# A hybrid decoder layer on one core: the mixer phase's mask cut in parts, its exponentials in three groups, the SSD step size moved into the exponent, and the gated norm split between w_out and ScalarE

## The chip, the cores and the metric

The kernel runs on one core of a Trainium2 chip. The metric is the device time of one execution in microseconds. The kernel before takes 3205.09 us in the median of three runs (3201.73 to 3206.28).

## What is computed

One decoder layer over 2048 tokens of width 1024 in float32. A combined projection feeds three token mixers: S5 (512 channels), Mamba-2 SSD (768 channels, 12 heads of 64, two B/C groups) and mLSTM (6 heads, key width 64, value width 128). Their outputs are concatenated (2048 wide), multiplied by `w_out`, normed and added to x, and a SwiGLU feed-forward follows. What the change touches is this:

```python
dt = softplus(dt_raw + dt_bias)
xdt = x * dt[..., None]
acs = cumsum(dt * a)                       # within a chunk of 128
decay = exp(where(causal, acs[l] - acs[s], -inf))
y_diag = einsum(cb, decay, xdt)            # cb = C B^T of the chunk
...
y = y_diag + y_off + x * d_skip
y = y * silu(z)
y = rmsnorm(y, norm_g)                     # over each of two groups of 384 channels
mix = concat[y_a, y_b, y_c] @ w_out
```

The mLSTM part has a causal matrix of exponentials of the same kind for its six heads.

## The kernel before, in words

The layer is five phases, one after the other, with a barrier between them: channels, tokens, mixers, out and feed-forward. Every float32 product of the big projections is made of three products of operands split in an upper and a lower part: ScalarE copies the upper part in a rounded type, VectorE subtracts it from the whole to get the lower part, and TensorE multiplies upper by upper, lower by upper and upper by lower.

**Tokens (`phase_tokens`).** TensorE runs through units of weights; each is loaded by SyncE, split by ScalarE (`upper`, L924) and VectorE (`lower`, L1003) and multiplied (L1126). At fixed slots between them `gates` computes the gates of the mixers for a quarter of the tokens, so four times in all: VectorE L1021 to L1054, ScalarE L941 to L952 (Exp and Ln), VectorE L1057 and L1058, then TensorE's transposes L1143. The row `col_b` (L1047) holds minus the cumulated decay of each head, and goes to the mixers as a column of `tok_cols`.

**Mixers (`phase_mixers`).** The 2048 tokens are 16 chunks of 128, with one loop over chunks written out by hand on every engine; semaphores count chunks. The order of work on each queue is the order in the code.

- SyncE loads for chunk c the rows `bc` (L1289, 18 rows of 128 numbers, spread to all partitions), `ch` (L1294), `va` (L1295), `tk` (L1297) and `zo` (L1300) into buffer c mod 2. All five raise one semaphore, `in_[b]`; each load waits for what its buffer was read by two chunks before: `bc` for the mLSTM product, `zo` for `y_ok`. Then, in the first three chunks, two pieces of `w_out` (L1305).
- GpSimd makes `xde` (L1402) and `xskip` (L1405), waits for VectorE's `off_read`, adds (L1407), makes `ve` (L1410), and adds the causal mask to all 18 heads of the next chunk in one instruction (`masked`, L1393), after a wait for all five loads.
- ScalarE copies three upper parts of the transposed y of the chunk before (`upper_y`, L1341), squares and sums y (L1326), takes the root by Ln and Exp (L1333, L1334), computes the 18 exponentials of the next chunk (`exponentials`, L1320), sends y, and moves out a finished product (L1354).
- VectorE waits for all exponentials, multiplies them by the products (L1449 for mLSTM, L1454 for SSD), makes `xdt` (L1457), scales the old states (L1458, L1459), reads the product with the old state (L1466), adds (L1474) and gates (L1475) the SSD output, updates states (L1479, L1495), forms the mLSTM output (L1482, L1490, L1498 to L1500, L1504 for six heads) and ends with the norm of y by root and gain (L1508, two instructions). Between these it makes the lower parts of the transposed y (`lower_y`, L1428), and in the first three chunks those of `w_out` (`lower_w`, L1422).
- TensorE has the products of the chunk (L1554 qk, L1560 cb, L1566 off, L1575 diag, L1583 state, L1591 inter, L1599 pv, L1606 c), twelve transposes of the chunk before (L1543), and between them in pieces the 36 matmuls of the projection of the chunk two before with half of `w_out` (`project`, L1529).

The order of TensorE around VectorE's exponent products:

```python
pe.wait_ge(gm_ok, 2 * c + 2)     # L1449, both
... off products, project(c - 2, 3, 4), transposes(c - 1, 0), project(c - 2, 4, 6)
pe.wait_ge(g_ok, 2 * c + 2)      # L1454, both
pe.wait_ge(xdt_ok, c + 1)
... diag products
```

**Out (`phase_out`).** It loads the rest of `w_out` in five groups of four row tiles into two buffers (L1652), splits them (L1711 on ScalarE, L1774 on VectorE), and multiplies (L1814); each group's load waits until the lower part of the group two before is made.

## Time and profile before

| what | value |
| --- | --- |
| median of three runs | 3205.09 us |
| time of the profiled execution | 3212.2 us |
| its span, first to last instruction | 3210.4 us |
| TensorE busy | 2919.7 us, 91% |
| VectorE busy | 1959.8 us, 61% |
| ScalarE busy | 1167.8 us, 36% |
| GpSimd busy | 372.4 us, 12% |
| mean granted TensorE clock | 0.955 |

Times are microseconds from the first instruction. PE is TensorE (PEld its weight load), DVE VectorE, ACT ScalarE, POOL GpSimd; a q behind a name is the engine's queue of issued DMAs. Where a row gives three numbers with slashes, they are the shortest, the median and the longest duration in ns. In a timeline a row is: start, duration, engine, line, operation, what it writes and reads, shape, count, and in brackets the idle time before it with what ended it. The mixers lie between about 1153 and 1635 us, tokens end at 1153, out begins at 1635. The profiled execution takes 1.8 us more than its span and 7.1 us more than the median.

### The profile page before, as it was taken

The numbers are of one execution on the slowest core, as the hardware profiler recorded it, in microseconds if no ns is written. First come the engines' busy times: TensorE is split into PE (matmuls) and PEld (weight loads), VectorE is DVE, ScalarE is ACT, GpSimd is POOL, SyncE is SP. The second block draws the span as 40 slices with busy tenths as digits, with TensorE's granted clock in tenths as the row PEclk, the third lists the DMA queues.
The fourth block names the chain that finished last, engine by engine and source line by source line (L and its number), as shares of the span: only waits on it lengthen the run. The fifth ranks groups of instructions, "written<-read, shape, count | busy, mean of one in ns | idle before, by whom it ended". The sixth has DMA issues, their size and how long they took to land. (4 is left out here: it accounts for less than half of the span.)

```text
span 3210.4 us, 35825 instructions
## 1 busy us (share of the span) xinstructions
PE 2919.7 (91%) x13608; PEld 2346.8 (73%) x13608; DVE 1959.8 (61%) x2603; ACT 1167.8 (36%) x1917; POOL 372.4 (12%) x415
## 2 busy tenths in 40 slices
PE   7999999789997846888869968999999999999998
PEld 4888887577775535666648856888878888888887
DVE  3777887556632218887823437676777655665756
ACT  5222222443433323333323334333343333354543
POOL 0000000004420014444401210000000000000000
PEclk9999999889998878999979988999999999999999
DMA  4222442336655455675456856344454222586863
GB/s 142 63 76 85 138 132 82 124 128 214 211 176 141 126 179 180 210 244 206 170 213 249 332 190 226 151 154 157 155 189 172 111 102 99 183 292 195 290 194 114
DMA packets 289959, 545.51 MB, mean 170 GB/s; under 512 B 58460, under 2 KB 150012, under 8 KB 276348
## 3 DMA queue, kind: packets, MB, share of 16 engines
q1 hardware_dynamic: 258028, 438.08, 40.5%
q0 software_dynamic: 24704, 75.52, 6.5%
q10 hardware_dynamic: 7056, 29.63, 2.3%
q8 instruction: 108, 1.77, 0.2%
q14 instruction: 63, 0.52, 0.1%
HBM read 358.69 MB, written 184.44 MB: 169 GB/s over the span
## 5 line engine op out<-in xcount | busy, mean ns | idle before, releaser
L2344 PE MATMUL f_banks<-f_bop,f_w_op 128*128 128x512 f32 x3696 | 840.4, 390 | 31.6 <-DVE f_w_op L2171 29.4
L2344 PEld LDWEIGHTS f_banks<-f_bop,f_w_op 128*128 128x128 f32 x3696 | 694.9, 188 | 177.1 <-DVE f_w_op L2171 29.8
L2352 PE MATMUL f_banks<-f_d_op 128*128 128x512 f32 x1848 | 419.0, 389 | 0.0
L2352 PEld LDWEIGHTS f_banks<-f_d_op 128*128 128x128 f32 x1848 | 347.0, 188 | 71.9
L1126 PE MATMUL t_banks<-t_w_hi,h_hi 128*128 128x512 f32 (+1 forms) x640 | 250.8, 392 | 31.9 <-DVE t_w_lo L1003 31.9
L2235 DVE TENSOR_TENSOR f_d_op<-f_d_raw,f_d_op 128x1024 fp32r<-128x1024 f32 x154 | 187.5, 1225 | 148.9 <-ACT f_d_op L2088 148.2
L639 PE MATMUL c_banks<-h_hi,c_w_hi 128*128 128x512 f32 x640 | 255.8, 400 | 0.0
L639 PE MATMUL c_banks<-h_hi,c_w_lo 128*128 128x512 f32 x640 | 249.9, 390 | 0.0
L639 PE MATMUL c_banks<-h_lo,c_w_hi 128*128 128x512 f32 x640 | 249.1, 389 | 0.0
L1126 PE MATMUL t_banks<-t_w_hi,h_lo 128*128 128x512 f32 (+1 forms) x640 | 240.8, 376 | 0.0
L1126 PE MATMUL t_banks<-t_w_lo,h_hi 128*128 128x512 f32 (+1 forms) x640 | 240.2, 375 | 0.0
L2088 ACT ACTIVATE f_d_op<-f_d_raw 128x1024 fp32r<-128x1024 f32 x154 | 162.9, 1061 | 198.3 <-PE f_banks L2352 161.6
L2070 ACT ACTIVATE f_snap<-f_banks 128x1024 f32<-128x1024 f32 x88 | 90.3, 1026 | 260.3 <-PE f_banks L2344 260.3
L1126 PEld LDWEIGHTS t_banks<-t_w_hi,h_hi 128*128 128x128 f32 x640 | 124.2, 194 | 64.0 <-DVE t_w_lo L1003 33.6
L894 POOL DMA_DIRECT2D tokmaj<-t_out x96 | 52.9, 553 | 980.5 <-ACT t_out L931 980.3
L2171 DVE TENSOR_TENSOR f_w_op<-f_w_sum,f_w_op 128x1024 fp32r<-128x1024 f32 x66 | 80.8, 1225 | 129.4 <-ACT f_w_op L2058 128.5
L1814 PE MATMUL o_banks<-o_w_hi,o_y_hi 128*128 128x512 f32 x320 | 129.3, 404 | 24.0 <-DMA o_y_lo<-y_lo 16.3
L1003 DVE TENSOR_TENSOR t_w_lo<-t_raw,t_w_hi 128x2048 fp32r<-128x2048 f32 x36 | 82.5, 2292 | 109.5 <-ACT t_w_hi L924 109.0
L418 DVE SCALAR_TENSOR_TENSOR c_arena<-c_row,c_cw,c_arena 128x512 f32<-128x512 f32 x192 | 144.3, 752 | 6.8
L1126 PEld LDWEIGHTS t_banks<-t_w_hi,h_lo 128*128 128x128 f32 x640 | 124.6, 195 | 23.5 <-issue 3.8
L1126 PEld LDWEIGHTS t_banks<-t_w_lo,h_hi 128*128 128x128 f32 x640 | 124.3, 194 | 21.6
L2171 DVE TENSOR_TENSOR f_w_op<-f_raw,f_w_op 128x1024 fp32r<-128x1024 f32 x88 | 107.8, 1225 | 52.4 <-ACT f_w_op L2058 50.2
(341 smaller groups left out, 4660.5 us busy)
## 6 DMA issues: line engine op xcount, KB each, us to landing
f_raw<-in_w_gu SPq DMA_DIRECT2D x88, 512.0 KB, 6.5
sop<-f_a SPq DMA_DIRECT2D x154, 256.0 KB, 2.0
f_d_raw<-sop SPq DMA_DIRECT2D x154, 256.0 KB, 2.9
t_raw<-in_w_tok SPq DMA_DIRECT2D x36, 1024.0 KB, 5.6
f_d_raw<-top SPq DMA_DIRECT2D x88, 256.0 KB, 4.1
m_bc<-rows SPq DMA_DIRECT2D x16, 1152.0 KB, 6.8
f_d_raw<-in_w_dn SPq DMA_DIRECT2D x66, 256.0 KB, 3.0
o_y_hi<-y_hi SPq DMA_DIRECT2D x16, 1024.0 KB, 5.0
```

The costliest lines, as they stand in the source:

```text
L418: ins = nc.vector.scalar_tensor_tensor(conv[:, s], row[:, s, k:NB + k], cw[:, m, k:k + 1], conv[:, s], ALU.mult, ALU.add)
L639: last = nc.tensor.matmul(banks[:, p % RING, :], w[:, n % 2, k, :], h[:, k, q * NB:(q + 1) * NB], start=k == 0 and j == 0, stop=k == KD - ...
L894: pool.dma_start(tokmaj_dram[tile * P:(tile + 1) * P, to:to + width], out[:, e % 2, first:first + width]).then_inc(out_sent[e % 2], 16)
L1003: tt(w_lo[:, unit % 2], raw[:], w_hi[:, unit % 2].bitcast(F32), sub).then_inc(wlo_ok, 1)
L1126: last = nc.tensor.matmul(banks[:, t, 0:width], h[:, k_first + k, tok], w[:, unit % 2, cols], start=begins and k == 0 and j == 0, stop=end ...
L1814: last = nc.tensor.matmul(banks[:, b, half, :], y[:, b, ky, :], w[:, k, :], start=ky == 0 and j == 0, stop=k in (KM - 1, KM + WG - 1) and ...
L2070: nc.scalar.activation(snap[:, slot], bank, ACT.Copy).then_inc(snap_ok, 1)
L2088: nc.scalar.activation(d_op[:, d % D_RING, 0:2], d_raw[:, d % S_RING], ACT.Copy).then_inc(dhi_ok, 1)
L2171: tt(w_op[:, t % W_RING, 1], src, w_op[:, t % W_RING, 0].bitcast(F32), sub).then_inc(wlo_ok, 1)
L2235: tt(d_op[:, d % D_RING, 2:4], d_raw[:, d % S_RING], d_op[:, d % D_RING, 0:2].bitcast(F32), sub).then_inc(dlo_ok, 1)
L2344: last = nc.tensor.matmul(bank[:, g, :], w_op[:, t % W_RING, w, cols], bop[:, s, h, k, :], start=begins and k == 0 and j == 0, stop=k == 3 ...
L2352: last = nc.tensor.matmul(banks[:, bank, :], d_op[:, d % D_RING, s, tok], d_op[:, d % D_RING, w, :], start=k == 0 and j == 0, stop=k == FU ...
```

## The change

In the tokens phase the SSD rows of `col_b` become ln(dt) minus the cumulated decay, so that the exponential holds the step dt and `xdt` is not made. In the mixers `bc` has a semaphore of its own, the mask is added in six instructions of three heads, ScalarE computes the exponentials in three groups at three places, the gain of the norm is multiplied into rows of `w_out` while these are split, and ScalarE multiplies y by the root.

```diff
@@ phase_tokens, ScalarE (r == 6), VectorE (r == 0) and (r == 7)
+                    chain(nc.scalar.activation(x[s_, :], x[s_, :], ACT.Ln))
                     chain(nc.scalar.activation(col_b[f, :], x[f, :], ACT.Exp))
...
+                    chain(ts(x[s_, :], sp_[s_, :], TINY, None, ALU.max))
                     chain(nc.vector.tensor_copy(decay[:, tiles], end))
...
+                    chain(tt(col_b[s_, :], x[s_, :], cum[s_, :], sub))
                     chain(ts(col_c[f, :], col_c[f, :], DK ** -0.5, None, mul))
@@ phase_mixers
-LOADS = 5
+LOADS = 4
+MH = 3
+MASKED = (12, 15, 0, 3, 6, 9)
+GK = XW // P
@@ SyncE
-            ... (gain[:], norm_gain.partition_broadcast(P)),
+            ... (gain[:], norm_gain),
-                             rows_dram[c]...partition_broadcast(P)).then_inc(in_[b], 16)
+                             rows_dram[c]...partition_broadcast(P)).then_inc(bc_in[b], 16)
@@ ScalarE
             def upper_w(g):
                 act.wait_ge(w_in[g % 2], 16 * (g // 2 + 1))
-                nc.scalar.activation(w_hi[:, WM * g:WM * (g + 1), :], w_raw[:, g % 2], ACT.Copy).then_inc(whi_ok, 1)
+                if WM * g < GK:
+                    for k in range(WM * g, WM * (g + 1)):
+                        ins = nc.scalar.activation(w_hi[:, k, :], w_raw[:, g % 2, k % WM], ACT.Copy, scale=gain[:, k:k + 1])
+                else:
+                    ins = nc.scalar.activation(w_hi[:, WM * g:WM * (g + 1), :], w_raw[:, g % 2], ACT.Copy)
+                ins.then_inc(whi_ok, 1)
             def exponentials(c, first, last):
-                act.wait_ge(mask_ok, c + 1)
                 for h in range(first, last):
+                    if h % MH == 0:
+                        act.wait_ge(mask_ok, NBC // MH * c + MASKED.index(h) + 1)
@@ norm(c), behind its wait for mean_ok
                 chain(nc.scalar.activation(stat[:, 2, :], stat[:, 1, :], ACT.Ln))
-                nc.scalar.activation(stat[:, 3, :], stat[:, 2, :], ACT.Exp, scale=-0.5).then_inc(rstd_ok, 1)
+                chain(nc.scalar.activation(stat[:, 3, :], stat[:, 2, :], ACT.Exp, scale=-0.5))
+                for g in range(NG):
+                    at = y[:, c % 2, g * GW:(g + 1) * GW]
+                    ins = nc.scalar.activation(at, at, ACT.Copy, scale=stat[:, 3, g:g + 1])
+                ins.then_inc(yn_ok, 1)
@@ ScalarE's loop over chunks
                     upper_y(c - 1, 0)
                     upper_y(c - 1, 1)
+                if c + 1 < TT:
+                    exponentials(c + 1, HS, NBC)
+                if 1 <= c <= TT:
                     upper_y(c - 1, 2)
+                if c < TT:
+                    squares(c)
+                if c + 1 < TT:
+                    exponentials(c + 1, 0, HG)
                 if c < TT:
                     norm(c)
                 if c + 1 < TT:
-                    exponentials(c + 1, 0, HS)
-                    exponentials(c + 1, HS, NBC)
+                    exponentials(c + 1, HG, HS)
@@ GpSimd
             def masked(c):
-                pool.wait_ge(in_[c % 2], (c // 2 + 1) * 16 * LOADS)
-                nc.gpsimd.tensor_tensor(bc[:, c % 2], bc[:, c % 2], mask[:]..., ALU.add).then_inc(mask_ok, 1)
+                pool.wait_ge(bc_in[c % 2], (c // 2 + 1) * 16)
+                for h in MASKED:
+                    part = bc[:, c % 2, h:h + MH]
+                    nc.gpsimd.tensor_tensor(part, part, mask[:]..., ALU.add).then_inc(mask_ok, 1)
...
+                pool.wait_ge(in_[b], (c // 2 + 1) * 16 * LOADS)
@@ VectorE
-                dve.wait_ge(expo_ok, 2 * c + 2)
+                dve.wait_ge(expo_ok, 3 * c + 1)
...
                 for g in range(NG):
+                    dve.wait_ge(expo_ok, 3 * c + 2 + g)
...
-                tt(xdt[:], x, over(col(c, 0, 0, HS), HD), mul).then_inc(xdt_ok, 1)
...
-                dve.wait_ge(rstd_ok, c + 1)
-                for g in range(NG):
-                    at = slice(g * GW, (g + 1) * GW)
-                    ins = stt(y[:, b, at], y[:, b, at], stat[:, 3, g:g + 1], gain[:, at], mul, mul)
@@ TensorE: transposes wait for yn_ok (n == 0) and y_ok (n == 1); diag reads tk in place of xdt
-                pe.wait_ge(xdt_ok, c + 1)
@@ phase_out: SyncE, between the loads of y and of w_out's second group
+            sp.dma_start(norm_col[:], norm_gain).then_inc(norm_in, 16)
```

VectorE's `lower_w` is cut in the same way as `upper_w`: for the first three of six groups one scalar_tensor_tensor of 128x512 for each row tile, raw times gain minus upper. In `phase_out` the row tiles 4 to 9 carry the gain, so groups 1 and 2 (of 0 to 4) are split by four instructions of 128x512 each on ScalarE and on VectorE, and group 1 waits for the column of gains.

## Rows read from the trace of the kernel before

**Rows 1.** Windows, chunks 3 to 14: stretch, busy PE, PEld, DVE, ACT, POOL; clock, DMA

```profile
1283.20:1590.10 306.90, 257.78 (x1584) 200.67 (x1584) 254.18 (x348) 109.14 (x337) 138.84 (x60) 0.93 0.62 217
```

**Rows 2.** Timeline of PE, ACT and DVE at the mixers' first chunk

```profile
1190.53 1.65 PE L1554 MATMUL m_bank_x<-m_ch 64*128 64x128 f32 x12 [36.94 <-DMA m_zo<-tokmaj]
1195.71 5.36 ACT L1320 ACTIVATE m_bc<-m_bc,m_tok_cols 128x128 f32<-128x128 f32 x18 [28.36 <-POOL m_bc L1393]
1201.21 1.02 DVE L1449 SCALAR_TENSOR_TENSOR m_bc<-m_bc,m_bank_x 128x384 f32<-128x384 f32 x2 [33.69 <-ACT m_bc L1320]
```

**Rows 3.** Timeline of DVE: L1449 of chunks 3 and 15, chunk 8; all L1493

```profile
1283.17 1.02 DVE L1449 SCALAR_TENSOR_TENSOR m_bc<-m_bc,m_bank_x 128x384 f32<-128x384 f32 x2 [0.44 <-ACT m_bc L1320]
...
1417.35 0.96 DVE L1466 TENSOR_TENSOR m_off<-m_bank_x,m_tok_cols 128x768 f32<-128x768 f32 x1
...
1421.35 1.17 DVE L1475 TENSOR_TENSOR m_y<-m_y,m_zo 128x768 f32<-128x768 f32 x1
...
1427.67 2.56 DVE L1493 TENSOR_SCALAR m_stat<-m_stat 128x2 f32<-128x2 f32 x1
...
1430.72 0.94 DVE L1498 SCALAR_TENSOR_TENSOR m_den<-m_num 128x6 f32<-128x6 f32 x1
1431.69 1.40 DVE L1499 TENSOR_TENSOR m_den<-m_den,m_tok_cols 128x6 f32<-128x6 f32 x1
...
1433.35 2.29 DVE L1504 SCALAR_TENSOR_TENSOR m_y<-m_num,m_den,m_zo 128x128 f32<-128x128 f32 x6
1435.67 1.27 DVE L1508 SCALAR_TENSOR_TENSOR m_y<-m_y,m_stat,m_gain 128x384 f32<-128x384 f32 x2
...
1590.13 1.02 DVE L1449 SCALAR_TENSOR_TENSOR m_bc<-m_bc,m_bank_x 128x384 f32<-128x384 f32 x2
...
L1493 DVE TENSOR_SCALAR m_stat<-m_stat x16: 169/310/2695, 1220.8 to 1607.2; 128x2 f32<-128x2 f32 x16
```

**Rows 4.** Timeline of POOL and DVE, chunks 8 and 9

```profile
1418.45 1.81 POOL L1407 TENSOR_TENSOR m_off<-m_off,m_xskip 128x768 f32<-128x768 f32 x1 [15.56 <-DVE m_off L1466]
...
1425.08 5.12 POOL L1393 TENSOR_TENSOR m_bc<-m_bc,m_mask 128x2304 f32<-128x2304 f32 x1 [3.37 <-DMA m_zo<-tokmaj]
1430.14 1.49 POOL L1402 TENSOR_TENSOR m_xde<-m_tk,m_tok_cols 128x768 f32<-128x768 f32 x1
1431.58 1.49 POOL L1405 TENSOR_TENSOR m_xskip<-m_tk,m_skip 128x768 f32<-128x768 f32 x1
...
1446.41 5.09 POOL L1393 TENSOR_TENSOR m_bc<-m_bc,m_mask 128x2304 f32<-128x2304 f32 x1
...
1447.43 4.89 DVE L1475 TENSOR_TENSOR m_y<-m_y,m_zo 128x768 f32<-128x768 f32 x1
```

**Rows 5.** Timeline of PE, from the off product of chunk 8 to that of 9

```profile
1413.31 1.56 PE L1566 MATMUL m_bank_x<-m_h,m_ch 128*128 128x384 f32 x4 [1.51 <-DVE m_bc L1449]
...
1432.93 0.39 PE L1529 MATMUL m_acc<-m_w_lo,m_y_hi 128*128 128x512 f32 x1
1438.05 2.50 PE L1566 MATMUL m_bank_x<-m_h,m_ch 128*128 128x384 f32 x4 [4.74 <-DVE m_bc L1449]
```

**Rows 6.** Timeline of DVE and POOL in chunk 0: two pairs side by side

```profile
1213.38 4.12 DVE L1422 TENSOR_TENSOR m_w_lo<-gate_rows,m_w_hi 128x1024 fp32r<-128x1024 f32 x1
...
1216.36 2.46 POOL L1402 TENSOR_TENSOR m_xde<-m_tk,m_tok_cols 128x768 f32<-128x768 f32 x1
```

**Rows 7.** Timeline of ACT and PE in the tokens phase, third round of gates

```profile
647.33 1.28 ACT L945 ACT_TABLE_LOAD   x1
...
670.66 1.28 ACT L948 ACT_TABLE_LOAD   x1
...
675.41 1.18 PE L1143 MATMUL t_side<-t_ident,t_arena 64*128 64x64 f32 x16 [3.17 <-issue]
```

**Rows 8.** Timeline of DVE in the out phase: one split, one 512-wide scalar_tensor_tensor

```profile
1661.67 2.29 DVE L1774 TENSOR_TENSOR o_w_lo<-o_w_raw,o_w_hi 128x2048 fp32r<-128x2048 f32 x1 [2.05 <-ACT o_w_hi L1711]
...
1682.90 0.75 DVE L1786 SCALAR_TENSOR_TENSOR o_work<-o_work,o_stat,o_gain_row 128x512 f32<-128x512 f32 x1 [0.64 <-ACT o_stat L1715]
```

More of the change, by code:

```diff
@@ L1225, in phase_mixers @@
         decay, decay_m = sb("m_decay", [P, HS, TT]), sb("m_decay_m", [P, HP, TT])
-        skip, gain, ident_sb = sb("m_skip", [P, HS]), sb("m_gain", [P, XW]), sb("m_ident", [P, P])
-        xdt, xde, xskip = (sb("m_" + s, [P, HS, HD]) for s in ("xdt", "xde", "xskip"))
+        skip, gain, ident_sb = sb("m_skip", [P, HS]), sb("m_gain", [P, GK]), sb("m_ident", [P, P])
+        xde, xskip = (sb("m_" + s, [P, HS, HD]) for s in ("xde", "xskip"))
         ve = sb("m_ve", [P, HM, DA])
@@ L1248, in phase_mixers @@
                                     "acc_mm"))
-        (xdt_ok, g_ok, gm_ok, off_read, diag_read, gated_ok, h_ok, inter_read, num_ok, c_ok, mean_ok, y_ok, ylo_ok) = (
-            sem("m_" + n) for n in ("xdt_ok", "g_ok", "gm_ok", "off_read", "diag_read", "gated_ok", "h_ok", "inter_read",
+        (g_ok, gm_ok, off_read, diag_read, gated_ok, h_ok, inter_read, num_ok, c_ok, mean_ok, y_ok, ylo_ok) = (
+            sem("m_" + n) for n in ("g_ok", "gm_ok", "off_read", "diag_read", "gated_ok", "h_ok", "inter_read",
                                     "num_ok", "c_ok", "mean_ok", "y_ok", "ylo_ok"))
-        (ssq_ok, rstd_ok, yhi_ok, part_ok, whi_ok, wlo_ok) = (
-            sem("m_" + n) for n in ("ssq_ok", "rstd_ok", "yhi_ok", "part_ok", "whi_ok", "wlo_ok"))
+        (ssq_ok, yn_ok, yhi_ok, part_ok, whi_ok, wlo_ok) = (
+            sem("m_" + n) for n in ("ssq_ok", "yn_ok", "yhi_ok", "part_ok", "whi_ok", "wlo_ok"))
+        bc_in = sem("m_bc_in0"), sem("m_bc_in1")
         const_in, in_, w_in = sem("m_const_in"), (sem("m_in0"), sem("m_in1")), (sem("m_w_in0"), sem("m_w_in1"))
@@ L1321, in exponentials, with squares @@
                 ins.then_inc(expo_ok, 1)
-            def norm(c):
+            def squares(c):
                 act.wait_ge(gated_ok, c + 1)
@@ L1358, in _ @@
             act.wait_ge(const_in, 16 * 7)
-            exponentials(0, 0, HS)
             exponentials(0, HS, NBC)
+            exponentials(0, 0, HG)
+            exponentials(0, HG, HS)
             for c in range(TT + 2):
@@ L1391, in masked @@
             def masked(c):
-                pool.wait_ge(in_[c % 2], (c // 2 + 1) * 16 * LOADS)
-                nc.gpsimd.tensor_tensor(bc[:, c % 2], bc[:, c % 2], mask[:].unsqueeze(1).to_broadcast([P, NBC, P]),
-                                        ALU.add).then_inc(mask_ok, 1)
+                pool.wait_ge(bc_in[c % 2], (c // 2 + 1) * 16)
+                for h in MASKED:
+                    part = bc[:, c % 2, h:h + MH]
+                    nc.gpsimd.tensor_tensor(part, part, mask[:].unsqueeze(1).to_broadcast([P, MH, P]), ALU.add
+                                            ).then_inc(mask_ok, 1)
             masked(0)
@@ L1421, in lower_w @@
                 dve.wait_ge(whi_ok, g + 1)
-                tt(w_lo[:, WM * g:WM * (g + 1), :], w_raw[:, g % 2], w_hi[:, WM * g:WM * (g + 1), :].bitcast(F32),
-                   ALU.subtract).then_inc(wlo_ok, 1)
+                if WM * g < GK:
+                    for k in range(WM * g, WM * (g + 1)):
+                        ins = stt(w_lo[:, k, :], w_raw[:, g % 2, k % WM], gain[:, k:k + 1], w_hi[:, k, :].bitcast(F32),
+                                  mul, ALU.subtract)
+                else:
+                    ins = tt(w_lo[:, WM * g:WM * (g + 1), :], w_raw[:, g % 2], w_hi[:, WM * g:WM * (g + 1), :].bitcast(F32),
+                             ALU.subtract)
+                ins.then_inc(wlo_ok, 1)
             def lower_y(c, n):
@@ L1572, in _ @@
                 pe.wait_ge(g_ok, 2 * c + 2)
-                pe.wait_ge(xdt_ok, c + 1)
                 for h in range(HS):
-                    last = mm(bank_y[:, h // HG, h % HG * HD:(h % HG + 1) * HD], bc[:, b, h, :], xdt[:, h, :],
+                    last = mm(bank_y[:, h // HG, h % HG * HD:(h % HG + 1) * HD], bc[:, b, h, :], tk[:, b, X_C + h * HD:X_C + (h + 1) * HD],
                               start=True, stop=True)
@@ L1710, in upper @@
                 act.wait_ge(w_in[g % 2], 16 * (g // 2 + 1))
-                nc.scalar.activation(w_hi[:, WG * g:WG * (g + 1), :], w_raw[:, g % 2], ACT.Copy).then_inc(whi_ok, 1)
+                if g == UT // WG:
+                    act.wait_ge(norm_in, 16)
+                if UT <= WG * g < UT + GK:
+                    for k in range(WG * g, WG * (g + 1)):
+                        scale = norm_col[:, k - UT:k - UT + 1] if k < UT + GK else 1.0
+                        ins = nc.scalar.activation(w_hi[:, k, :], w_raw[:, g % 2, k % WG], ACT.Copy, scale=scale)
+                else:
+                    ins = nc.scalar.activation(w_hi[:, WG * g:WG * (g + 1), :], w_raw[:, g % 2], ACT.Copy)
+                ins.then_inc(whi_ok, 1)
             def factor(n, at, rstd):
@@ L1773, in _ @@
                 dve.wait_ge(whi_ok, g + 1)
-                tt(w_lo[:, WG * g:WG * (g + 1), :], w_raw[:, g % 2], w_hi[:, WG * g:WG * (g + 1), :].bitcast(F32),
-                   ALU.subtract).then_inc(wlo_ok, 1)
+                if UT <= WG * g < UT + GK:
+                    for k in range(WG * g, WG * (g + 1)):
+                        scale = norm_col[:, k - UT:k - UT + 1] if k < UT + GK else 1.0
+                        ins = stt(w_lo[:, k, :], w_raw[:, g % 2, k % WG], scale, w_hi[:, k, :].bitcast(F32), ALU.mult, ALU.subtract)
+                else:
+                    ins = tt(w_lo[:, WG * g:WG * (g + 1), :], w_raw[:, g % 2], w_hi[:, WG * g:WG * (g + 1), :].bitcast(F32),
+                             ALU.subtract)
+                ins.then_inc(wlo_ok, 1)
             dve.wait_ge(const_in, 48)
```

22 lines of the change are left out of this document (12 added, 10 removed).

## The prediction

> **What bounds the kernel now.** I read first the windows, then the timelines of each engine around one chunk, then the waits' brackets in them. The mixers are what the change aims at, so I look for what sets their pace. Over chunks 3 to 14 TensorE is busy 257.8 of 306.9 us, VectorE 254.2, ScalarE 109.1 and GpSimd 138.8, with DMAs at a share of 0.62 [rows 1]: two engines near 84% and neither full, so the pace is set by waits between them. VectorE's first exponent product L1449 starts at 1283.17 in chunk 3 and at 1590.13 in chunk 15 [rows 3], so a chunk takes 306.96 / 12 = 25.6 us.
>
> TensorE alone would need less. From the off product of chunk 8 (1413.31) its matmuls follow one another up to the last projection before the next off product, which starts at 1432.93; with the 0.23 us at which these follow it is free at 1433.2. That is 19.9 us of work in a chunk at nearly full clock, and then it waits 4.74 us for VectorE's L1449 [rows 5]. So the loop runs through VectorE, and I call P the start of the off product and count from it.
>
> VectorE's own work would allow 19.1: L1493 starts at P + 14.4, behind the pv product; from there to L1504 it takes 5.68 us, of which most is not work. L1493 takes 2.56 us where its shortest is 0.17, and the tiny L1498 and L1499 take 0.94 and 1.40 [rows 3]; I take 0.17 for these too. The excess is 2.39 + 0.77 + 1.23 = 4.4 us. Each of the three ends when a GpSimd instruction ends: the mask (1425.08 + 5.12 = 1430.20), then xde (1431.63), then xskip (1433.07) [rows 4]. In chunk 9 the mask starts at 1446.41 instead and the gate product L1475 beside it takes 4.89 us, against 1.17 in chunk 8 [rows 3, 4]. VectorE thus stands still while a GpSimd instruction runs, if its own operands are all in SBUF; the 5.1 us mask in one piece is the costliest cover. Then come L1504 (2.29 us), L1508 (1.27 us) and L1449.
>
> At the start of the phase everything waits for loads. TensorE begins at 1190.53, when zo has landed, ScalarE at 1195.71, after the mask, and VectorE at 1201.21, after all 18 exponentials (5.36 us) [rows 2].
>
> **The change, part by part: chunks 3 to 14.** *Norm and xdt off VectorE.* L1508 stands in the loop between L1504 and L1449: minus 1.27 us, and the small waits for ScalarE before L1449 (0.44 in chunk 3 [rows 3]) go too, since the exponentials come earlier. xdt (L1457, a 128x768 product; by its neighbour of that size L1466, 0.96 us) is in the loop only on paper. The sum L1474 waits for TensorE's diag products, and these stand in its queue behind off, a transpose group and three pieces of projection: L1475, right behind it, starts at 1421.35, P + 8.0 [rows 3], and this order stays. I give xdt nothing, but VectorE's off_read comes 0.9 us earlier, at P + 4.1 (now 1417.35 + 0.96 = P + 5.0 [rows 3, 5]), and GpSimd starts so much earlier. What is late next there is TensorE.
>
> *The mask in parts.* No row shows a mask of 384 numbers a partition. From below it is a sixth of 5.12, 0.85 us. From L1407 (768 numbers, 1.81) and the mask (2304, 5.12) [rows 4] a number costs (5.12 - 1.81) / 1536 = 2.15 ns, and a part 1.81 - 384 x 0.00215 = 0.98 us. I take 0.98, as both rows are in-place additions on this engine, and six are 5.9. After off_read GpSimd needs 1.81 for L1407 and some 1.5 for ve (the size of xde), so parts start at P + 7.4, with no wait for zo any more. L1475, ready at P + 8.0, waits for the end of the running part (P + 8.4), not for the whole mask; the next part waits for it, 1.0 us. The mask ends at P + 14.3, xde at 15.8, xskip at 17.3.
>
> *VectorE's small instructions.* L1493 is ready at P + 14.4, falls behind xde and ends at 15.8: a wait of 1.4. With L1495 (0.6 us by the gap between its neighbours) L1498 is ready at 16.4 and waits 0.9 for xskip. So 2.3 of the 4.4 us stay. P' = P + 19.1 (without L1508) + 2.3, less the rounding of small gaps, is P + 21.2. TensorE's 19.9 stay below it. Gain: 25.6 - 21.2 = 4.4 a chunk, 52.8 in twelve. If parts cost 0.85, GpSimd is 0.8 us ahead and the loop is 20.4; at 1.15 it is a microsecond longer, 22.2.
>
> *ScalarE.* It gets two copies of 128x384, some 1 us, and computes the first six exponentials ahead of the third copy of y. Its wait for parts 1 and 2 ends at P + 10.5, six exponentials take 5.36 / 3 = 1.8 us [rows 2] and overlap part 2, so it copies at about P + 11.4, when TensorE's transposes are done anyway; the projection is covered. It is busy 109 of 307 us [rows 1], and I cost its part at nothing. That cover goes if a part takes over 1.5 us. Behind its new place in the queue are the squares, the norm and the last six exponentials: done by P + 18.6, and L1454 wants these at about P' + 0.8.
>
> *SyncE and DMAs.* The order of loads stays and y_ok is earlier by L1508. At 0.62 of 25.6 us DMAs are busy 15.9 us in a chunk [rows 1], which fits in 21.2: cost nothing.
>
> **Start and first chunks.** With its own semaphore bc, issued ahead of four other loads, can be masked before zo lands. Then L1449 follows TensorE's qk products at 1190.53 + 1.65 = 1192.2, not 1201.2: minus 9.0. If bc lands together with zo it is some 5. I take 9.0, since four loads stand behind bc in the same queue. In chunks 0 to 2 the loop also holds the lower parts of w_out, one of which took 4.12 us beside the mask [rows 6]; four pieces of 0.75 (the 512-wide one [rows 8]) now take turns with parts. L1508's 1.27 is sure there, 4.4 is the most; I take 3.2 a chunk, 9.6.
>
> **Tokens.** Four added Ln, each between 0.3 us, one exponential of 128 numbers (5.36 / 18 [rows 2]), and 1.2, four of them, for its 512; I take 0.65. And before Exp another table: the trace has a load of 1.28 us for Ln at 647.33 and one for Exp at 670.66, with only copies between [rows 7], so the Ln's table serves no Exp and three rounds get a load more. That round's transposes waited 3.17 us for this chain [rows 7] and get it whole: 0.65 for Ln and 0.7 for the new subtraction. I count 0.9 for each of the other three, where the chain has more room. Plus 4 us, between 0 (the weight loads, which TensorE waits for next, take it in) and 7, when each round pays the 1.35 and the VectorE operation ahead of a split 0.4. The Trainium skill (ScalarE: Activation LUTs, "Table sets: the hidden batching unit") has Ln then Exp in one load, since one set holds both; by it three loads of 1.28 would not come and the sum would be some 1.5 us lower. The trace speaks against it for the tables chosen here.
>
> **Out.** Two splits of 2.29 become eight of 0.75 [rows 8]: 1.4 more on VectorE, in a chain load, split, next load, for which TensorE waits. Plus 1.5, between 0 and 3 with ScalarE's four pieces.
>
> **Sum:** 52.8 + 9.6 + 9.0 - 4 - 1.5 = 65.9. The profiled execution would go from 3212.2 to 3146; it lies 7.1 above the median, and the median goes from 3205.1 to 3139.
>
> **The rivals.** *TensorE becomes the bound.* If small instructions slip between GpSimd's, the loop is 19.9: 12 x 5.7 = 68, 9 + 13 at the start, less 2 for the other phases: 88, so 3117. For it: the stall-free 19.1 is below TensorE's work. Against: xde and xskip still end the GpSimd block just when L1493 comes.
>
> *The stall moves.* If VectorE loses about as much as now (4.4 us) to six parts and two products, the loop is 19.1 + 4.4 = 23.5 and twelve chunks give 25; with 9 + 6 and less 6 it is 34, so 3171. For it: total GpSimd work rises from 5.1 to 5.9 and starts earlier in the chunk.
>
> *Locked out, slower.* The place is L1475. If GpSimd's parts follow so closely that VectorE gets no turn, L1475 waits for all six: with parts of 0.98 it ends at P + 14.4 and the state update that pv needs at about 16. TensorE has pv and then at least 6.5 us: pv ends before L1490, a microsecond ahead of L1493, so by P + 13.4 of 19.9. That gives about P + 24. It is slower than before only if parts also take over some 1.2 us; at 1.5, with a microsecond of low clock after the wait, it is 28.1, or 12 x 2.5 - 9 + 5.5 = 26.5 more: 3232. Against it: in chunk 0 VectorE's L1422 waited for a GpSimd instruction, and GpSimd's next, xde, then took 2.46 us where it takes 1.49 alone [rows 4, 6]: turns were taken. The Trainium skill (SBUF — State Buffer, "SBUF: two separate sides") calls the shared port pair an exclusive lock that whoever starts first holds for its whole instruction, and promises no turn; as far as the holding goes the rows agree.
>
> *Not what it says.* If bc lands as late as zo and the groups only move waits, the start gives 5 or less; that is inside my range.
>
> **How the numbers follow.** Forecast 0.54, TensorE bound 0.19, stall moves 0.21, locked out 0.05, and 0.01 for the unforeseen. The range goes from 3115, just below the TensorE case, to 3172, just above the moved stall. A measurement of this kernel can tell about 0.2% (6.4 us) from no change. Faster by more than that: 0.93; within: 0.03; slower: 0.04.
>
> **What would show it.** Right: L1449's period near 21 us, parts near 0.98 us, L1475 under 2.2 us in every chunk, L1449 of chunk 0 within 2 us of TensorE's first qk product, TensorE's wait before the off product about 1.3 us. Wrong: L1475 of 4 us and more, parts over 1.2 us, a wait for zo or tk by GpSimd at xde, or ScalarE's third copy of y waiting for mask parts with TensorE idle behind it.

## The result, and the profile after

The changed kernel takes 3131.42 us in the median of four runs (3131.07 to 3133.67), the kernel before, run beside it, 3205.69 (3201.73 to 3208.56, four runs). The ratio is 0.9771, with a 95% interval of 0.9754 to 0.9788. The forecast was 3139 in a range of 3115 to 3172. The span of the profiled execution goes from 3210.4 to 3129.3 us, by 81.1; that is more than the 74.3 between the medians, since the profiled execution of the kernel before lay above its median.

Over chunks 3 to 14, in the windows' columns of [rows 1], TensorE is now busy nearly all the time, and the granted clock is 1.00 in place of 0.93:

```profile
1260.22:1510.00 249.78, 241.27 (x1592) 189.98 (x1590) 207.78 (x313) 126.29 (x360) 151.70 (x120) 1.00 0.79 273
```

The timeline of VectorE gives the period, the time from one chunk's first exponent product to the next one's. L1484 is the first exponent product, L1449 before; L1508 the gate product (was L1475), L1526 the mean (L1493), L1531 and L1532 the small denominator operations (L1498, L1499), L1537 the six outputs (L1504). The rows show chunks 3, 8 and 15; they answer to [rows 3].

```profile
1260.20 1.02 DVE L1484 SCALAR_TENSOR_TENSOR m_bc<-m_bc,m_bank_x 128x384 f32<-128x384 f32 x2
...
1373.18 1.56 DVE L1508 TENSOR_TENSOR m_y<-m_y,m_zo 128x768 f32<-128x768 f32 x1
...
1379.81 1.15 DVE L1526 TENSOR_SCALAR m_stat<-m_stat 128x2 f32<-128x2 f32 x1
1380.88 0.55 DVE L1528 TENSOR_TENSOR m_c<-m_c_old,m_bank_y 128x387 f32<-128x387 f32 x1
1381.45 0.94 DVE L1531 SCALAR_TENSOR_TENSOR m_den<-m_num 128x6 f32<-128x6 f32 x1
1382.43 0.17 DVE L1532 TENSOR_TENSOR m_den<-m_den,m_tok_cols 128x6 f32<-128x6 f32 x1
1382.63 0.19 DVE L1533 RECIPROCAL m_den<-m_den 128x6 f32<-128x6 f32 x1
1382.86 2.29 DVE L1537 SCALAR_TENSOR_TENSOR m_y<-m_num,m_den,m_zo 128x128 f32<-128x128 f32 x6
1385.18 1.02 DVE L1484 SCALAR_TENSOR_TENSOR m_bc<-m_bc,m_bank_x 128x384 f32<-128x384 f32 x2
...
1509.98 1.02 DVE L1484 SCALAR_TENSOR_TENSOR m_bc<-m_bc,m_bank_x 128x384 f32<-128x384 f32 x2
```

(1509.98 - 1260.20) / 12 = 20.8 us a chunk, where it was 25.6: 57.2 us less in twelve chunks. The timelines of GpSimd and TensorE in chunk 8 (answering to [rows 4, 5]; L1422 is the mask in six parts, L1432 xde, L1435 xskip, L1597 the off product):

```profile
1369.72 1.81 POOL L1437 TENSOR_TENSOR m_off<-m_off,m_xskip 128x768 f32<-128x768 f32 x1 [8.15 <-DVE m_off L1499]
1371.49 1.48 POOL L1440 TENSOR_TENSOR m_ve<-m_va,m_tok_cols 128x774 f32<-128x774 f32 x1
1372.93 6.57 POOL L1422 TENSOR_TENSOR m_bc<-m_bc,m_mask 128x384 f32<-128x384 f32 x6
1379.46 1.47 POOL L1432 TENSOR_TENSOR m_xde<-m_tk,m_tok_cols 128x768 f32<-128x768 f32 x1
1380.90 1.47 POOL L1435 TENSOR_TENSOR m_xskip<-m_tk,m_skip 128x768 f32<-128x768 f32 x1
```

```profile
1365.45 1.56 PE L1597 MATMUL m_bank_x<-m_h,m_ch 128*128 128x384 f32 x4 [0.77 <-DVE m_bc L1484]
```

As in the prediction, P is the start of TensorE's off product in a chunk; here it is 1365.45. The mask starts at P + 7.5 with no wait for a load, and the gate product (P + 7.7) gets its turn after the first part: 1.56 us, where chunk 9 before lost 4.89. In single rows five parts take 1.00 to 1.04 us, and the second, which stands beside the gate product, 1.73. TensorE's wait before the off product is 0.77 us (4.74 before).

The start of the phase, in the timelines of GpSimd, TensorE and VectorE (answering to [rows 2]):

```profile
1180.74 5.75 POOL L1422 TENSOR_TENSOR m_bc<-m_bc,m_mask 128x384 f32<-128x384 f32 x6 [16.07 <-DMA m_bc<-rows]
1187.52 1.65 PE L1585 MATMUL m_bank_x<-m_ch 64*128 64x128 f32 x12 [36.26 <-DMA m_zo<-tokmaj]
1189.42 1.02 DVE L1484 SCALAR_TENSOR_TENSOR m_bc<-m_bc,m_bank_x 128x384 f32<-128x384 f32 x2 [24.22 <-PE m_bank_x L1585]
```

Where the 81.1 us of span went, by the first and last rows of each stretch: start of L1449 or L1484 in chunk 0, 1201.2 to 1189.4, 11.8; chunks 0 to 2, 82.0 to 70.8, 11.2; twelve chunks, 57.2; from chunk 15 to the last matmul of the mixers, 44.7 to 43.1, 1.6; TensorE's stretch in out, 259.3 to 257.4, 1.9; and 2.6 lost in the feed-forward phase and the gap before out.

### The profile page after: what moved, and what is told of

It is laid out like the page before. It is cut to its first block and busy times, and to the rows that moved or that the text cites. A ratio compares the mean times of both kernels' runs of the same rounds, so it can differ in the third digit from the quotient of the medians.

```text
span 3129.3 us, 35939 instructions
## 1 busy us (share of the span) xinstructions
PE 2893.2 (92%) x13608; PEld 2329.2 (74%) x13608; DVE 1905.5 (61%) x2572; ACT 1198.4 (38%) x1965; POOL 389.7 (12%) x495
## 5 line engine op out<-in xcount | busy, mean ns | idle before, releaser
L895 POOL DMA_DIRECT2D tokmaj<-t_out x96 | 52.8, 552 | 978.1 <-ACT t_out L932 978.1
L2217 DVE TENSOR_TENSOR f_w_op<-f_w_sum,f_w_op 128x1024 fp32r<-128x1024 f32 x66 | 80.8, 1225 | 129.4 <-ACT f_w_op L2104 128.6
L1130 PEld LDWEIGHTS t_banks<-t_w_hi,h_lo 128*128 128x128 f32 x640 | 123.2, 193 | 23.5 <-issue 3.8
L640 PEld LDWEIGHTS c_banks<-h_hi,c_w_lo 128*128 128x128 f32 x640 | 120.1, 188 | 26.0
L640 PEld LDWEIGHTS c_banks<-h_hi,c_w_hi 128*128 128x128 f32 x640 | 120.2, 188 | 25.5 <-issue 2.4
```

The source lines that it names most:

```text
L640: last = nc.tensor.matmul(banks[:, p % RING, :], w[:, n % 2, k, :], h[:, k, q * NB:(q + 1) * NB], start=k == 0 and j == 0, stop=k == KD - ...
L895: pool.dma_start(tokmaj_dram[tile * P:(tile + 1) * P, to:to + width], out[:, e % 2, first:first + width]).then_inc(out_sent[e % 2], 16)
L1130: last = nc.tensor.matmul(banks[:, t, 0:width], h[:, k_first + k, tok], w[:, unit % 2, cols], start=begins and k == 0 and j == 0, stop=end ...
L2217: tt(w_op[:, t % W_RING, 1], src, w_op[:, t % W_RING, 0].bitcast(F32), sub).then_inc(wlo_ok, 1)
```

## The experiments

The kernel before took 3201.8 us beside the first four runs, 3208.8 beside the second four and 3204.2 (median of nine, 3193.9 to 3209.1) beside the last four. Single runs are read by the period of a chunk, from the first exponent product of chunk 3 to that of chunk 15, which their traces give to 0.1 us. Theory: the loop's pace is set by VectorE operations that wait for a running GpSimd instruction, and the change pays by what it takes out from behind them. Rivals: TensorE sets the pace already; or the parts of the change are independent savings.

### One part undone at a time

**Mask in one instruction again** (`a_mask_whole`).

```diff
-                for h in MASKED:
-                    part = bc[:, c % 2, h:h + MH]
-                    nc.gpsimd.tensor_tensor(part, part, mask..., ALU.add).then_inc(mask_ok, 1)
+                nc.gpsimd.tensor_tensor(bc[:, c % 2], bc[:, c % 2], mask..., ALU.add).then_inc(mask_ok, 1)
```

> The changed kernel with the mask in one instruction again, all else as changed. Theory (VectorE stands still while a GpSimd instruction runs, so the length of one instruction is what costs): the gate product waits from P + 8 for the whole mask and takes about 5 us instead of 1.6, the state update comes near P + 15, TensorE has 8.1 us of work behind it, and the period goes from 20.8 to 23 to 24.5 us, the time to about 3170 us. Rival (the mask's pieces don't matter, the gain is that of the norm and of the exponentials): period 20.8 to 21.2, time 3131 to 3137 us.

Measured: 3186.96 us, period 24.7. The rival falls; the loss is somewhat above my range. Timelines of GpSimd (L1420) and VectorE (L1506, the gate product) in chunk 8:

```profile
1401.99 5.08 POOL L1420 TENSOR_TENSOR m_bc<-m_bc,m_mask 128x2304 f32<-128x2304 f32 x1
...
1402.50 5.39 DVE L1506 TENSOR_TENSOR m_y<-m_y,m_zo 128x768 f32<-128x768 f32 x1
```

The gate product is ready half a microsecond after the mask started and ends 0.82 us after it. In every one of chunks 3 to 14 it is ready 0.2 to 0.5 us after the mask's start and stands behind all of it.

**xdt back on VectorE** (`a_xdt_back`), with the step out of the exponent.

```diff
+                tt(xdt[:], tk[...], over(col(c, 0, 0, HS), HD), mul).then_inc(xdt_ok, 1)
...
+                pe.wait_ge(xdt_ok, c + 1)
```

> The changed kernel with xdt made by VectorE again, in its old place, and the exponent without ln(dt). Theory (xdt isn't in VectorE's own loop, as the sum waits for TensorE's diag products, but it moves GpSimd's block of mask, xde and xskip 0.9 us later, and VectorE's tiny instructions wait for its end): period 20.8 + 0.9 = 21.7 us, time about 3144 us, with the wait moved to the last tiny instruction. Rival (xdt is hidden behind the diag products): period 20.8, time 3131 us give or take the tokens phase.

Measured: 3138.22 us, period 21.5. In chunk 8 (P = 1370.1) GpSimd's block starts 0.9 us later and a third small operation, L1533, falls behind xskip. Timelines of GpSimd and VectorE:

```profile
1378.45 6.57 POOL L1419 TENSOR_TENSOR m_bc<-m_bc,m_mask 128x384 f32<-128x384 f32 x6
...
1386.41 1.48 POOL L1432 TENSOR_TENSOR m_xskip<-m_tk,m_skip 128x768 f32<-128x768 f32 x1
```

```profile
1384.44 0.61 DVE L1527 TENSOR_SCALAR m_stat<-m_stat 128x2 f32<-128x2 f32 x1
...
1386.52 1.39 DVE L1533 TENSOR_TENSOR m_den<-m_den,m_tok_cols 128x6 f32<-128x6 f32 x1
```

So the 0.95 us of xdt are worth nothing where they stood, and 0.7 a chunk through the time at which GpSimd starts.

**Norm's product back on VectorE** (`a_norm_dve`): the two `ACT.Copy` of `norm(c)` are left out, and two scalar_tensor_tensor of 128x384 come behind the outputs.

```diff
+                for g in range(NG):
+                    at = slice(g * GW, (g + 1) * GW)
+                    ins = stt(y[:, b, at], y[:, b, at], stat[:, 3, g:g + 1], ones[:], mul, mul)
```

> The changed kernel with the multiplication of y by the root back on VectorE, two instructions of the old shape at the end of the chunk, ScalarE's two copies gone. Theory (VectorE's loop is the bound and the two stand in it): period 20.8 + 1.3 = 22.1 us, time about 3150 us. Rival (another engine sets the pace and this was moved for nothing): period within 0.3 us of 20.8, time within 5 us of 3131.

Measured: 3155.55 us, period 22.4; chunks take 22.1, and every second or third 22.8. The added pair takes 1.27 us and stands in the loop, as in [rows 3]. The 22.8 are chunks in which the sum comes at P + 8.4 in place of 6.7 and all behind it is late; in each of them the off product took 1.76 to 2.93 us, in the others 1.56.

**All exponentials behind the norm** (`a_exps_late`).

```diff
-                if c + 1 < TT:
-                    exponentials(c + 1, HS, NBC)
...
-                    exponentials(c + 1, 0, HG)
@@ behind norm(c)
+                    exponentials(c + 1, HS, NBC)
+                    exponentials(c + 1, 0, HG)
                     exponentials(c + 1, HG, HS)
```

> The changed kernel with all three groups of exponentials behind squares and norm, in the same order. Theory: the mLSTM group ends near P + 19, before VectorE wants it at 19.7, but the last SSD group ends near P + 22.5 and the last SSD product starts a microsecond late; TensorE's diag products don't notice, GpSimd's block does, so the period is 21.6 to 21.8 us and the time about 3144 us. Rival (exponentials are the pace as a block): period 23.5 us, time 3170 us. Rival (they are hidden wherever they stand): 20.8 us, 3131 us.

Measured: 3135.79 us, period 21.2, alternating 20.8 and 21.6. Every second chunk behaves as expected, the others lose nothing: 4.4 us in all, not 13.

**One semaphore for all loads** (`a_one_sem`): GpSimd's mask waits for bc, ch, va, tk and zo again.

```diff
-                pool.wait_ge(bc_in[c % 2], (c // 2 + 1) * 16)
+                pool.wait_ge(in_[c % 2], (c // 2 + 1) * 16 * LOADS)
```

> The changed kernel with bc on the semaphore of the other loads again, so that the mask waits for zo. Theory: at the start the mask begins when zo has landed, and chunk 0 is 4 to 5 us later; in the steady chunks zo lands at about P + 7.5 to P + 12 while GpSimd wants to begin at P + 7.5, so the mask waits 0 to 4 us and the period is 21 to 23 us. Time 3140 to 3160 us. Rival (the semaphore pays at the start alone): period 20.8, time 3135 us.

Measured: 3173.87 us, period 23.1: at my range's end for the period and above it for the time, since tokens ended 5.7 us later here and chunks 0 to 2 take 80.8 (70.8 in the changed kernel). The start itself loses little: L1484 of chunk 0 comes 3.2 us after TensorE's first qk product, in place of 1.9. GpSimd's timeline in chunk 9 (P = 1417.3) shows the wait for zo; at the faster pace it is longer than in [rows 4]:

```profile
1429.42 5.83 POOL L1421 TENSOR_TENSOR m_bc<-m_bc,m_mask 128x384 f32<-128x384 f32 x6 [4.57 <-DMA m_zo<-tokmaj]
```

### One part done alone, in the kernel before

**The mask in six parts** (`b_mask_parts`; the diff is the first one turned round, with ScalarE's wait for all six).

> The kernel before with nothing changed but the mask, cut in six parts. Theory: in the chunks whose mask starts right behind ve the gate product takes 1.6 us instead of 4.9 and the period falls by some 3 us; in those whose mask waits for zo all exponentials still wait for its last part, at about P + 18, and the period stays near 24.5. Mean 23.5 us instead of 25.6, time about 3178 us. Rival (six turns cost as much as one wait): 25.6 us, 3205 us.

Measured: 3182.81 us, period 24.0. The gate product takes 0.96 to 1.78 us everywhere; but a mask that waits for zo starts near P + 11, and xde and xskip run from P + 16 to P + 20, beside outputs and small operations.

**bc's own semaphore** (`b_own_sem`).

```diff
-LOADS = 5
+LOADS = 4
...
-                pool.wait_ge(in_[c % 2], (c // 2 + 1) * 16 * LOADS)
+                pool.wait_ge(bc_in[c % 2], (c // 2 + 1) * 16)
```

> The kernel before with nothing changed but a semaphore of its own for bc. Theory: the start is 9 us earlier, but now every chunk's mask begins right behind ve, and every gate product waits for the whole of it, as in every second chunk before, where the period was 26.8 us on average against 24.5 in the others. Period 26 to 27 us, time 3195 to 3215 us. Rival (an earlier mask is good in every chunk): period 24.5 to 25, time about 3185 us.

Measured: 3177.21 us, period 23.9. My expectation was wrong in its sign. I had the mask start always at P + 8.4 and the gate product always behind it. The timelines of GpSimd (L1394) and VectorE (L1477), chunks 7 and 8:

```profile
1375.50 5.08 POOL L1394 TENSOR_TENSOR m_bc<-m_bc,m_mask 128x2304 f32<-128x2304 f32 x1
...
1401.32 5.84 POOL L1394 TENSOR_TENSOR m_bc<-m_bc,m_mask 128x2304 f32<-128x2304 f32 x1
```

```profile
1376.45 4.94 DVE L1477 TENSOR_TENSOR m_y<-m_y,m_zo 128x768 f32<-128x768 f32 x1
...
1401.01 1.17 DVE L1477 TENSOR_TENSOR m_y<-m_y,m_zo 128x768 f32<-128x768 f32 x1
```

In chunk 8 the gate product is ready 0.3 us before the mask: it takes 1.17, the mask waits for it, and the chunk takes 22.7 us. In chunk 7 it is ready 0.95 us after the mask's start, waits for all of it, and the chunk takes 25.8. What makes it late is TensorE: its off product of chunk 7, after a wait of 2.68 us, runs at half the clock, and the gate product comes 1.3 us later after P (9.3 for 8.0). Windows (columns of [rows 1]) at the off products of chunks 7 and 8:

```profile
1367.14:1370.10 2.96, 2.96 (x5) 1.75 (x6) 2.96 (x4) 0.00 (x0) 0.00 (x0) 0.50 1.02 417
...
1392.96:1396.00 3.04, 3.04 (x14) 2.25 (x15) 3.04 (x4) 0.32 (x1) 0.00 (x0) 1.00 1.07 414
```

**The step in the exponent** (`b_step_exp`): xdt and its wait are left out.

> The kernel before with nothing changed but the step size in the exponent and xdt gone. Theory: where the mask follows ve, it and the gate product behind it come 0.9 us earlier; where it waits for zo, nothing changes: mean period 25.1 us, 6 us less in all, and the tokens phase 0 to 4 us longer by its Ln and table loads; time 3198 to 3205 us. Rival (xdt's 0.9 us count in every chunk): 24.7 us, 3191 us or less. Rival (the tokens phase gains from something): its end is earlier than in the kernel before.

Measured: 3197.57 us, period 24.8, with TensorE's last tokens matmul at 1155.8 in place of 1153.6. The period is the rival's, the time lies between the two.

Alone the three give 26, 32 and 11 us, each from one run beside one run of the kernel before. Undone from the changed kernel (3131.4) five parts cost 55.5 (mask), 42.4 (semaphore), 24.1 (norm), 6.8 (step) and 4.4 (exponentials): 133 together, where the whole change gives 74. Each of these is one run too, but the sum is too far above 74 for that to matter, and the periods say the same (3.9, 2.3, 1.6, 0.7 and 0.4 us a chunk, 8.9 together, where the whole change gives 4.8). So they aren't independent savings. Early bc makes the mask meet the gate product, and in these runs only parts make that meeting cheap (a wait does it as well, see below); parts alone still start late. The norm and the order of the exponentials were not tried alone in the kernel before.

### Is it the length of the instruction, or its place?

**Mask whole, gate product first** (`a_gate_first`), and **mask whole in the same order without that wait** (`a_whole_order`). In both ScalarE copies y and takes the squares before the exponentials.

```diff
+                if c >= 1:
+                    pool.wait_ge(gated_ok, c)
+                nc.gpsimd.tensor_tensor(bc[:, c % 2], bc[:, c % 2], mask..., ALU.add).then_inc(mask_ok, 1)
...
```

> The changed kernel with the mask in one instruction again, but in another order: GpSimd starts the mask of the next chunk only after the gate product of this one (a wait of its own for that), and ScalarE copies the third quarter of y and takes the squares before it waits for the mask instead of behind the exponentials. Theory: what a long GpSimd instruction costs is that VectorE's gate product stands behind all of it; with the gate product first (0.96 us, from 7.7 to 8.7 us after the off product's start) and the mask from 8.9 to 14.0 beside VectorE's work that reads PSUM, nothing waits, and the period is 20.8 us as with six parts: 3131 us, within 5. Rival: a GpSimd instruction of 5.1 us costs VectorE wherever it stands, since the mean and the denominator's small operations come to it late: 23 us or more, 3160 us or more.

> The kernel of the run before this one without GpSimd's wait for the gate product: mask in one instruction, ScalarE's copy and squares ahead of the exponentials. Theory: the gate product stands behind the whole mask again (5.4 us) but ScalarE is no longer late behind it: period near 23 us, 3160 us, and the difference to the earlier run with a whole mask (24.74 us, 3187 us) is what ScalarE's queue cost there. Rival: 24.7 us and 3187 us as there, so that all of it is the gate product's wait.

Measured: 3135.88 us and period 20.7 with the wait, 3184.32 us and 24.76 without. VectorE (L1507) and GpSimd (L1421) with the wait, chunk 8 (P = 1373.1):

```profile
1380.81 0.96 DVE L1507 TENSOR_TENSOR m_y<-m_y,m_zo 128x768 f32<-128x768 f32 x1
...
1387.43 1.05 DVE L1525 TENSOR_SCALAR m_stat<-m_stat 128x2 f32<-128x2 f32 x1
```

```profile
1381.91 5.12 POOL L1421 TENSOR_TENSOR m_bc<-m_bc,m_mask 128x2304 f32<-128x2304 f32 x1 [1.31 <-DVE m_y L1507]
```

One instruction of 5.1 us costs no more than six parts in chunks 3 to 14 if the gate product has gone first, and 4 us a chunk more if not. The 4.5 us between the first of these runs and the changed kernel lie in chunks 0 to 2 (76.7 against 70.8), where the splits of w_out stand beside the mask as well: the four pieces of chunk 0 take 8.27 us there and 5.62 in the changed kernel. ScalarE's queue was no part of `a_mask_whole`'s loss: the second theory of `a_whole_order` falls, and its rival holds (24.76 against 24.74).

### The two waits that were left

**xskip behind the outputs** (`a_xskip_late`), and **that with the mean folded into the logarithm** (`a_both`).

```diff
                 if c >= 1:
                     pool.wait_ge(offs_ok, c)
+                    pool.wait_ge(y_ok, c)
                 step(pool, nc.gpsimd.tensor_tensor(xskip[:], ...
@@ norm(c), in the second kernel only; L1526 and its wait are left out
-                chain(nc.scalar.activation(stat[:, 2, :], stat[:, 1, :], ACT.Ln))
+                chain(nc.scalar.activation(stat[:, 2, :], stat[:, 0, :], ACT.Ln, scale=1.0 / GW, bias=eps[:]))
```

> The changed kernel with one edit: GpSimd's copy of the D skip also waits for the outputs of the chunk before, so it does not stand in front of the small denominator operation. Theory: the mean's product still waits for xde (to about 15.5 us after the off product's start), the denominator operation then waits for nothing; outputs start at 16.6 instead of 17.4, period 20.0 to 20.1, about 3119 to 3121 us. If the run without the mean's product is no faster than this one, TensorE is the bound of both. Rival: 20.8 us and 3131 us as the changed kernel has, since the copy of the skip is not what the period hangs on.

> The changed kernel, with two edits meant to help VectorE. GpSimd's copy of the D skip now also waits for the outputs of the chunk before, so that it no longer stands in front of the small denominator operation; and the 0.35 us product that turns the sum of squares into a mean is left out on VectorE, its factor and its epsilon given to ScalarE's logarithm as scale and bias. Theory: the tail of a chunk is still set by waits of VectorE's small operations for GpSimd's copies. Without the mean the denominator operation stands first and waits for xde (ends some 15.6 us after the off product's start); the outputs start near 16.1 instead of 17.4, by 1.3 us, and TensorE's own floor of 19.9 to 20.0 us takes over from VectorE: period 20.0, 0.8 us by 15 chunks less, about 3119 us. Rival 1: the period is TensorE's already, 20.8 as in the changed kernel, 3131 us. Rival 2: the D skip, started later, is late for the next work of GpSimd or holds VectorE's outputs: 21 us or more, above 3134 us.

Measured: 3122.36 us (3118.57 to 3124.66, four runs), ratio to the kernel before 0.9747 (0.973 to 0.9765), period 20.05; and 3119.02 us (3115.68 to 3128.09, five runs), ratio 0.9742 (0.9722 to 0.9763), period 19.75. In the first, VectorE's small operations (timeline, chunk 8, P = 1363.5):

```profile
1377.86 1.17 DVE L1527 TENSOR_SCALAR m_stat<-m_stat 128x2 f32<-128x2 f32 x1
1378.94 0.55 DVE L1529 TENSOR_TENSOR m_c<-m_c_old,m_bank_y 128x387 f32<-128x387 f32 x1
1379.52 0.17 DVE L1532 SCALAR_TENSOR_TENSOR m_den<-m_num 128x6 f32<-128x6 f32 x1
...
1380.15 2.29 DVE L1538 SCALAR_TENSOR_TENSOR m_y<-m_num,m_den,m_zo 128x128 f32<-128x128 f32 x6
```

L1532 takes 0.17 in place of 0.94. In the second kernel TensorE has no gap left in twelve chunks (window, chunks 3 to 14):

```profile
1262.70:1499.70 237.00, 237.00 (x1586) 189.87 (x1586) 184.35 (x301) 125.77 (x360) 152.28 (x120) 1.00 0.80 279
```

In this kernel TensorE bounds the loop: VectorE's chain alone would be 19.5 (outputs at P + 16.07, 2.29 for these, 1.1 up to the next P). In `a_xskip_late` TensorE is idle for only 0.3 us in twelve chunks as well, but VectorE's chain still adds up to the whole 20.05 (outputs at P + 16.65), so there the two bounds nearly meet. Both are faster than the kernel before by more than a measurement's uncertainty. They weren't run beside the changed kernel, and the intervals of all three ratios overlap; that they beat it rests on their periods (20.8, 20.05 and 19.75, or 9 and 13 us in twelve chunks) and on medians 9 and 12 us lower.

## Why the prediction was right

The likeliest case came, and by its mechanism: a stall of VectorE behind GpSimd was most of what stood between the loop and TensorE's work.

- **Chunks 3 to 14.** Forecast 52.8, measured 57.2. Parts of 0.98 us were 1.00 to 1.04, the mask ended at P + 14.05 (forecast 14.3), xde at 15.5 (15.8), the gate product waited 0.6 us where up to one was allowed. The step that was mis-sized is VectorE's tail. I had 19.1 us stall-free plus 2.3 of waits. Chunk 15, which has no mask beside it, starts its outputs at P + 16.1 (P is 1511.06 there); with 2.29 for these and 1.1 up to the next P that is 19.5. Its rows in VectorE's timeline:

```profile
1525.94 0.56 DVE L1528 TENSOR_TENSOR m_c<-m_c_old,m_bank_y 128x387 f32<-128x387 f32 x1 [0.35 <-PE m_bank_y L1636]
...
1527.16 2.29 DVE L1537 SCALAR_TENSOR_TENSOR m_y<-m_num,m_den,m_zo 128x128 f32<-128x128 f32 x6
```

  The waits add 1.3, not 2.3. The mean's wait is 0.98, but only 0.55 of it count: behind the mean stands L1528, which TensorE's c product holds until P + 14.85 anyway (chunk 15, and `a_both`, which has no mean), and which the mean's wait puts at P + 15.4. The denominator's wait is 0.77 (forecast 0.9). 19.5 + 1.3 = 20.8. Some 0.4 of each error has one cause, a wait for TensorE hidden beneath the stall of the kernel before, and this part cancels. The other 0.6 of the overestimated waits is made up of three small things: xde ended 0.3 earlier, the mean's own 0.17 was counted as a wait, and the denominator waited 0.13 less. So the forecast came somewhat closer than its two terms.
- **A reading that was incomplete.** For the 4.89 us of the gate product in chunk 9 the prediction names the mask's early start alone. But [rows 4, 5] also show the gate product ready at P + 9.4 there and at P + 8.0 in chunk 8, and the off product at 2.50 us against 1.56. In all six odd chunks from 3 to 13 of the kernel before, TensorE had waited 3.1 to 4.9 us, the off product took 2.3 to 2.9, and the gate product was ready at P + 9.3 to 10.4, about a microsecond or more behind the start of a mask at P + 8.4; in the even ones it was ready at P + 8.0, ahead of that. What this lateness costs without any mask beside it shows in chunk 15 of the kernel before. Timelines of TensorE and VectorE:

```profile
1591.20 2.06 PE L1566 MATMUL m_bank_x<-m_h,m_ch 128*128 128x384 f32 x4 [4.35 <-DVE m_bc L1449]
...
1608.94 2.29 DVE L1504 SCALAR_TENSOR_TENSOR m_y<-m_num,m_den,m_zo 128x128 f32<-128x128 f32 x6
```

The outputs start at P + 17.7, 1.6 us later than the P + 16.1 of the changed kernel. If the 1.6 us counted in full in the six odd chunks, they would be 10 of the 57.2 us; if the lateness also cost the turn each time, some 4 us a chunk, since the odd chunks took 26.7 us on average and those of `b_own_sem` in which the gate product came first 22.7. Both are estimates, and no run holds the clock apart from the stall. That the mask is enough by itself shows in `a_mask_whole`: there the off product took 1.45 us in every one of chunks 3 to 14, and the gate product still stood behind the mask.
- **xdt** was worth nothing in its place and paid through off_read, as forecast; its size is 0.7 us a chunk in `a_xdt_back`.
- **The norm off VectorE**, 1.27 us a chunk in the forecast: 1.6 by `a_norm_dve`, of which 1.3 are its own (chunks of 22.1) and the rest lies in the chunks with a slow off product.
- **The order of the exponentials** I costed at nothing on ScalarE and credited with the small wait before L1449; `a_exps_late` gives 0.4 us a chunk.
- **Start.** Forecast 9.0 from bc's semaphore. From TensorE's first qk product to the first exponent product it was 10.7 us and is 1.9: 8.8. But I gave it all to the semaphore, and it isn't the semaphore's alone: alone it brings the 10.7 down to 3.8 (`b_own_sem`), and without it parts and groups bring it to 3.2 (`a_one_sem`), a gain of 7.5, where I had allowed 5 in place of 9. Parts without groups give nothing there (11.4 in `b_mask_parts`). The other 3.0 of the 11.8 are 2.3 of tokens that ended earlier (scatter and no gain of the change, see below) and 0.7 of loads.
- **Chunks 0 to 2.** Forecast 9.6, measured 11.2. **From chunk 15 on** I had counted nothing; it gave 1.6.
- **Tokens.** Forecast plus 4; in the two profiled executions the phase ended 2.3 us *earlier*. This is scatter. With the old gates code its last matmul ends at 1149.8 to 1153.6 (four traces, mean 1151.2), with the new at 1151.3 to 1157.0 (ten traces, mean 1153.4): plus 2.3, which the scatter makes uncertain by about a microsecond. The added Ln's table serves no Exp, as I argued from [rows 7]. Grouped rows of ScalarE and its timeline in the third round of gates:

```profile
L949 ACT ACT_TABLE_LOAD x3 | 3.8, 1283 | 0.1
```

```profile
672.36 0.61 ACT L949 ACTIVATE t_arena<-t_arena 12x512 f32<-12x512 f32 x1
672.99 1.28 ACT L950 ACT_TABLE_LOAD   x1
```

The load for Ln comes in three rounds, one for Exp follows in all four. By the Trainium skill (ScalarE: Activation LUTs, "Table sets: the hidden batching unit") Ln then Exp is one load, since one set holds both; in the tokens phase the trace disagrees, and 3 x 1.28 us of loads are new. In the mixers, where the code asks for that set before the loop, no load stands between Ln and Exp.

- **Out.** Forecast plus 1.5 for eight pieces of 0.75. Four splits take 2.74 us together and not 3.0, against 2.29 whole. TensorE's stretch in out lasts 258.5 us on average with the new code (ten traces, 257.3 to 259.5) and 257.2 with the old (four, 255.9 to 259.3): plus 1.3, though the profiled pair shows minus 1.9.

Of the rivals, *TensorE becomes the bound* was named with 19.9 us; its floor exists (19.75) but two small waits kept the loop a microsecond above it. *The stall moves* would have shown 23.5. *Locked out* was settled by the first part's turn; what it would have cost is seen in `a_mask_whole`, where the forecast's 24 us a chunk are 24.7.

## What to carry to other kernels

When an engine's small operations take a microsecond or more where their shortest takes 0.17, look which instruction of another engine ends at the same moment, and then ask which of the two should go first; a wait of its own in front of the long instruction (`a_gate_first`) did as much for the steady loop as cutting it. Look as well at why the late one is late: in the kernel before, the gate product stood behind the mask only in chunks with a slow off product. Parts of such a change can't be priced one by one, since an earlier start is worth something or nothing by what it meets. Under a stall may lie another wait, and a stall-free sum must be taken from a stretch where the stall is absent (here the last chunk), not from the stalled one minus its excess.
